# Attention steps of two heads from each key group, with score products that alternate between the two halves of the array's rows

## What is computed

```
proj = h @ w_in + b_in                     # 16 query heads, 2 key/value heads, 64 wide
q = q.reshape(B, NB, 128, Hkv, G, dh) * dh ** -0.5        # Hkv = 2 groups of G = 8 heads
kc, vc = with_prev(k), with_prev(v)        # a block sees itself and the one before: 256 keys
s = einsum('bnqhgd,bnkhd->bnhgqk', q, kc)  # scores, masked to a window of 128
mx = maximum(max(s, -1), sink)             # one learned sink logit per head
p = exp(s - mx)
p = p / (sum(p, -1) + exp(sink - mx))
o = einsum('bnhgqk,bnkhd->bnqhgd', p, vc).reshape(B, S, Hq * dh)
return o @ w_out + b_out
```

## Time and profile before

| | |
|---|---|
| runs | 1165.36, 1166.43, 1445.92 us; median 1166.43 |
| span of the profiled execution | 1163.4 us (its own time is not given) |
| PE busy | 1142.8 us, 98% |
| DVE, ACT busy | 543.2 us (47%), 431.8 us (37%) |
| mean granted TensorE clock | 0.998 of full speed |
| moved by DMA | 105.06 MB, 90 GB/s over the span |

### The profile page before, as it was taken

The page is one execution under the profiler, slowest core; times in us unless marked ns, Lnnn a source line. Parts: engine busy times, 40 slices in busy tenths (PEclk is TensorE's granted clock), DMA queues, the critical chain, the costliest instruction groups (busy, mean ns, idle before and its releaser), DMA issues.

```text
span 1163.4 us, 15354 instructions
## 1 busy us (share of the span) xinstructions
PE 1142.8 (98%) x5833; PEld 966.2 (83%) x5833; DVE 543.2 (47%) x834; ACT 431.8 (37%) x748; POOL 13.3 (1%) x22
## 2 busy tenths in 40 slices
PE   6999999999999999999999999999999999999997
PEld 6888888898888888888889988889888888888886
DVE  5424467854434434433365565555534434433344
ACT  6410325543332332323354365544332332323242
POOL 0000001000000000000000000000000000000000
PEclk9999999999999999999999999999999999999999
DMA  8233212323233233122262522002333233212241
GB/s 238 58 91 91 69 59 73 109 73 95 86 108 97 83 108 102 43 82 99 90 181 57 161 74 73 1 1 73 109 108 103 78 108 104 76 52 93 90 145 72
DMA packets 142855, 105.06 MB, mean 90 GB/s; under 512 B 22054, under 2 KB 130784, under 8 KB 142816
## 3 DMA queue, kind: packets, MB, share of 16 engines
q1 hardware_dynamic: 142816, 104.52, 30.1%
HBM read 102.41 MB, written 2.10 MB: 90 GB/s over the span
## 4 chain that ended last, share of the span: by engine, by line
PE 93%; DVE 3%; ACT 2%; DMA 1%; issue 0%; SPq 0%; DVEq 0%; ACTq 0%
PE ps L1298 18%; PE ps L1300 18%; PE ps L1299 18%; PE ps L1534 6%; PE ps L1535 6%; PE ps L1533 6%; PE ps L1611 2%; PE ps L1638 2%; PE ps L1478 2%; PE ps L1480 2%; PE ps L1479 2%; PE ps L1363 1%; PE ps L1365 1%; PE ps L1364 1%; PE ps L1622 1%; PE ps L1434 1%
## 5 line engine op out<-in xcount | busy, mean ns | idle before, releaser
L1298 PE MATMUL ps<-act_hi,w_hi 128*128 128x512 f32 (+1 forms) x1072 | 387.7, 362 | 1.4 <-DVE act_lo L841 1.4
L1299 PE MATMUL ps<-act_lo,w_hi 128*128 128x512 f32 (+1 forms) x1072 | 385.3, 359 | 0.0
L1300 PE MATMUL ps<-act_hi,w_lo 128*128 128x512 f32 (+1 forms) x1072 | 385.2, 359 | 0.0
L1298 PEld LDWEIGHTS ps<-act_hi,w_hi 128*128 128x128 f32 x1072 | 202.8, 189 | 33.4 <-DVE act_lo L841 2.2
L1299 PEld LDWEIGHTS ps<-act_lo,w_hi 128*128 128x128 f32 x1072 | 202.9, 189 | 29.9
L1300 PEld LDWEIGHTS ps<-act_hi,w_lo 128*128 128x128 f32 x1072 | 202.8, 189 | 30.0
L1533 PE MATMUL ps<-w_hi 128*128 128x512 f32 x288 | 112.0, 389 | 0.0
L1534 PE MATMUL ps<-w_lo,w_hi 128*128 128x512 f32 x288 | 112.0, 389 | 0.0
L1535 PE MATMUL ps<-w_hi,w_lo 128*128 128x512 f32 x288 | 112.0, 389 | 0.0
L664 ACT ACTIVATE arena<-ps,vecs 128x512 f32<-128x512 f32 x44 | 34.3, 779 | 188.9 <-PE ps L1300 188.9
L489 ACT CAST w_hi<-raw 128x1024 fp32r<-128x1024 f32 x71 | 73.4, 1046 | 81.6 <-PE ps L1300 45.0
(11 more groups left out here) (167 smaller groups left out, 1228.0 us busy)
## 6 DMA issues: line engine op xcount, KB each, us to landing
raw<-in_f_w_up SPq DMA_DIRECT2D x88, 512.0 KB, 4.3
raw<-in_f_w_down SPq DMA_DIRECT2D x44, 512.0 KB, 3.3
raw<-in_m_w_in SPq DMA_DIRECT2D x24, 512.0 KB, 3.8
raw<-in_m_w_out SPq DMA_DIRECT2D x8, 512.0 KB, 3.3
raw<-in_a_w_in SPq DMA_DIRECT2D x16, 256.0 KB, 4.4
raw<-in_a_w_out SPq DMA_DIRECT2D x8, 512.0 KB, 4.4
h<-in_x SPq DMA_DIRECT2D x4, 512.0 KB, 5.1
out<-h SPq DMA_DIRECT2D x3, 512.0 KB, 2.6
```

What stands on the lines that cost most here:

```text
L1298: nc.tensor.matmul(dst, lh, rh, start=(i == 0), stop=False)
L1299: nc.tensor.matmul(dst, lh, rl, start=False, stop=False)
L1300: last = nc.tensor.matmul(dst, ll, rh, start=False, stop=(i == n - 1))
```

## The change

A step takes the query tiles 2n and 2n + 1 of its block (n = s % 4), that is heads 2n, 2n + 8, 2n + 1 and 2n + 9 in this order, so its score products go to rows 0 to 63, 64 to 127, 0 to 63, 64 to 127. Key group g writes bank g. The sinks are read with a stride, each head of the mix takes its own group's values, and `o_tok` holds the heads in the order of the steps. So the rows of the output projection's weights are loaded in that order, by two DMAs of 64 rows each for a unit instead of one of 128, and `DMAS` counts two.

```
-    for q in [G_GATE] + [G_AIN + n for n in range(A_UNITS) if A_TILE[n] < KT]:
+    for q in [G_GATE] + [G_AIN + n for n in range(A_UNITS) if A_TILE[n] < KT] \
+            + [G_AOUT + k for k in range(KT)]:
         DMAS[q] = 2
...
-        GROUPS = [0, 2, 1, 3]
+        def pair(s, j):
+
+            return s // ASTEPS, s % ASTEPS * 2 + j // KVH, j % KVH
...
                 load_free(G_AOUT + k)
-                load(G_AOUT + k, a_w_out[0, k * P:(k + 1) * P])
+                s = SLOT[G_AOUT + k] % 4
+                for g in range(KVH):
+                    r0 = (k + KT * g) * DH
+                    nc.sync.dma_start(raw[g * DH:(g + 1) * DH, s], a_w_out[0, r0:r0 + DH])\
+                        .then_inc(raw_in[s], 16)
...
             def sink_cols(s):
-                n = GROUPS[s % ASTEPS]
-                return sink[:, n * AG:(n + 1) * AG]
+                n = s % ASTEPS
+                return sink[:].rearrange("p (g t) -> p t g", g=KVH)[:, 2 * n:2 * n + 2]
+
+            def by_pair(cols):
+                return cols.rearrange("p (t g) -> p t g", g=KVH)
...
                 for j in range(AG):
+                    _, t, g = pair(s, j)
+                    h0 = t + KT * g
                     ins = nc.vector.tensor_tensor_reduce(
-                        out=sc[:, b, j, lo:], in0=ps[:, j // 2, (j % 2) * 2 * P + lo:(j % 2 + 1) * 2 * P],
-                        in1=band[:, lo:], scale=DH ** -0.5, scalar=sink_cols(s)[:, j:j + 1],
+                        out=sc[:, b, j, lo:],
+                        in0=ps[:, g, (t % 2) * 2 * P + lo:(t % 2 + 1) * 2 * P],
+                        in1=band[:, lo:], scale=DH ** -0.5, scalar=sink[:, h0:h0 + 1],
                         op0=ALU.add, op1=ALU.max, accum_out=asm[:, b, 0, j:j + 1])
                 link(ins)
-                nc.vector.tensor_tensor(asm[:, b, 3], sink_cols(s), asm[:, b, 0], ALU.subtract)
+                nc.vector.tensor_tensor(by_pair(asm[:, b, 3]), sink_cols(s), by_pair(asm[:, b, 0]),
+                                        ALU.subtract)
...
             def scores(s):
-                blk, n = s // ASTEPS, GROUPS[s % ASTEPS]
-                g = n * AG // KT
-                pr = slice(g * DH, (g + 1) * DH)
+                blk = s // ASTEPS
...
                 for j in range(AG):
-                    t = (n * AG + j) % KT
-                    dst = ps[:, j // 2, (j % 2) * 2 * P + lo:(j % 2 + 1) * 2 * P]
+                    _, t, g = pair(s, j)
+                    pr = slice(g * DH, (g + 1) * DH)
+                    dst = ps[:, g, (t % 2) * 2 * P + lo:(t % 2 + 1) * 2 * P]
...
             def mix(s):
-                b, blk, n = s % 2, s // ASTEPS, GROUPS[s % ASTEPS]
-                g = n * AG // KT
+                b, blk = s % 2, s // ASTEPS
...
                 for j in range(AG):
+                    g = pair(s, j)[2]
```

More of the change, by code:

```diff
@@ L1228, in normalised @@
             def normalised(s):
-                b, blk, n = s % 2, s // ASTEPS, GROUPS[s % ASTEPS]
+                b, blk, n = s % 2, s // ASTEPS, s % ASTEPS
                 dve.wait_ge(pv_mm, s + 1)
```

## The result

The changed kernel takes 1156.11 us (median of 4 runs, 1154.79 to 1156.15), the kernel before 1166.08 in the same comparison. The ratio is 0.9912, 95% interval 0.9898 to 0.9927: 10.0 us less by the medians, where the prediction had 7.7. The median of the kernel before counts one execution of 1445.92 us; without it, it is 1165.73, and the first set too shows 9.6 us less. The profiled execution took 1156.1 us for a span of 1154.3, 1.8 us above it.

What follows compares the result with a forecast made beforehand. PE, busy 98% of the span, was taken as the bound; 7.74 us less from overlapping score passes, all else 0, took the span from 1163.4 to 1155.7, time 1158.7 us (chance 0.50), range 1156 to 1168.

Steps and rivals of the forecast that it cites:

- part 1: Score products alternating between row halves: passes overlap, a stretch falls from 1.92 to 1.28 us, 7.74 us over 12 steps.
- No overlap: Rival for the score passes: both halves share one stream, 0.215 us a pass stays, time 1166.4; chance 0.18.
- late weights: Rival for the score passes: a half's first weight load starts late, halving the overlap, time 1162.4; chance 0.15.
- an emptying at each change of half: Rival in the score stretch: 0.20 us three times a step, 9.6 us lost, time 1176.0; chance 0.14.
- starts stay in order: Assumption for the score passes: starts keep program order, so eight passes need five slots of 0.215 us, 0.645 less a step.
- Block 0: Its four steps with 128-column score passes: loads as long as streams, so no gain, stretch still about 1.1 us.
- overlapping loads: Rival: weight loads of different halves overlap too, block 0 included, 1.3 us more gain, time 1157.4; chance 0.03.
- part 3: Whether DVE and ACT keep up: ACT's copy before the mix has 0.81 us slack, 0.17 left, so the saving holds.
- part 4: Loads of w_out, 16 of 256 KB for 8 of 512 KB: each unit some 0.4 us later, covered, cost 0.
- part 5: DVE's strided read of sink columns, once a step: even at 0.48 us covered by 0.67 us of slack.
- The offset of 3.0 us: Median time 1166.43 taken as 3.0 above the profiled span of 1163.4, added to the forecast span of 1155.7.
- about 2%: Difference a measurement of this kernel tells from no change (1143 and 1190 us); within it 0.98.

Runs made afterwards that it cites:

- the run with the halves in turn: Changed kernel with a step's score products in head order 0, 2, 1, 3, four passes in rows 0 to 63, then four in 64 to 127: 1155.98 us.
- second set: The changed kernel measured again, unedited, beside the kernel before: 1155.69 us against 1165.31, ratio 0.9917.
- the run with the late mix: Changed kernel with a step's mix put behind the first unit of that step's output products, where there are any: 1158.46 us, ratio 0.9939.

## Why the prediction was right and wrong

- **What bounds the kernel, and that the scores count one to one:** right. PE stays busy 98%, and 10.2 us less between the first and last score pass make a span 9.1 shorter with a start 1.0 later.
- **Overlap of the two halves at all (part 1):** right, and the rivals fall. No overlap and late weights would have left stretches of 1.92 and 1.6 us, an emptying at each change of half over 2.4; it is 1.06. The exposed load and the emptying at the change of shape stayed: 1.06 is 0.105 + 4 x 0.215 + 0.095.
- **The size of the overlap: the step that failed.** The step was "starts stay in order", from which I counted five slots for U U L L U U L L. The passes fill four, because each half works through its own products and does not wait for the other's; the order of the program inside a step is free, as the run with the halves in turn shows. The term was 3 x 0.215 = 0.645 us a step and measured 0.86; over 12 steps 10.3 us, not 7.74. The range went wrong with it: its lower end, 1156, was built on five slots, and 1156.11 just lies in it while the second set's 1155.69 does not. (A reading beside it was loose too: eight starts have seven distances, of 0.126 us on average with the longer first one, not 0.110. The last start, 126.05, is right all the same.)
- **Block 0: wrong.** I put the gain at nothing, since loads and streams are equally long there, and gave overlapping loads 0.03 of chance and 1.3 us as upper end. The loads of the two halves do overlap: 0.45 us in each of four steps, 1.8 in all, more than that upper end, again because four slots remain and not five.
- **The cover on ACT (part 3): the number was right, and the larger saving went past it.** I had 0.81 us of slack before the mix and wrote that past it the copy would be the bound. With 0.86 it is. Between the first and the last score pass that returns 0.11 us in eight steps and 0.1 in two of block 0 (whose 0.39 us of slack I had not counted), 1.1 us; once more it comes behind the last. The other 0.8 lies in steps 6 and 7, where the stage hangs on ACT and DVE (copy, exponentials, act_hi, act_lo, then L1224), as the chain shows:

```profile
687.02 1.01 ACT arena L740
...
690.60 0.69 DVE act_lo L1259
...
693.53 2.08 ACT arena L731 x8
...
696.08 1.01 ACT arena L740
697.09 0.04 issue
697.13 2.00 PE ps L1651 x16
```

  From the one copy to the next this takes 9.1 us. In the kernel before, the same two copies start 9.1 us apart as well:

```profile
689.29 1.01 ACT L733 COPY arena<-ps 128x1024 f32<-128x1024 f32 x1 [2.31 <-PE ps L1622]
...
697.88 0.56 ACT L740 CAST act_hi<-ps 128x512 fp32r<-128x512 f32 x1
698.43 1.01 ACT L733 COPY arena<-ps 128x1024 f32<-128x1024 f32 x1
```

  There too the second copy began as soon as the act_hi cast ahead of it was done. So in this stretch ACT and DVE had no slack even before, and part 3, which looked at one later step and at the sum of ACT's busy time, missed it. In the page's chain over the whole span DVE has 4% and ACT 3% now, in place of 3% and 2%.
- **The loads (part 4) and DVE's strided read (part 5):** cost 0, right (L1230 takes 0.16 us as L1217 did). That the second unit would be 0.4 us later was wrong: it is 1.7 with the two DMAs alone and 2.1 in the changed kernel, because I counted only the issues and took the transfers to be as fast as before.
- **The sum:** 12.1 gross less 1.9 given back is 10.2; I had 7.7 gross and nothing back. Two errors of opposite sign, of which the first was the larger; that they partly cancel is luck. The offset of 3.0 us between span and time was too large as well: in the executions on record it is 1.7 to 1.9, in the kernel before too, so its span of 1163.4 belongs to an execution of some 1165.2 us (an estimate), below the three times given with it.
- **What a measurement can tell:** I said about 2%. The comparison resolved 0.9912 to within 0.15%, so a gain under 1% stands clear of the scatter.

The Trainium skill (TensorE: Matmul & The Clock Gate, "Part 3: Packing small matmuls") has starts about 4 ns apart for tiles in distinct row groups. The starts within 0.01 us here agree with it. The same part says that products start in strict program order. For products in different halves the measurement decides against it: in the run with the halves in turn, a pass starts ahead of three others that stand before it in the program.

## What to carry to other kernels

Products with 64 rows of contraction stream in half the time here if, between two changes of shape, the two halves of the rows have equally many of them (they also wrote different PSUM banks), and that where weight loads set the pace too; the 0.20 us of the changes of shape stay. Two orders among them gave the same time. Before counting the gain, take the smallest slack behind the shortened stretch and compare it with the largest gain, not the likeliest, and look at every step for it, not at one. Where an evacuation then becomes the bound, try releasing it by halves before moving PE's work: here it gained 2.3 us, while the work that was moved had been filling another wait.

## What the runs showed of the hardware that I had not expected

- Two f32 products in different halves of the rows run side by side at full speed, 256 columns in 0.215 us a pass each, and two weight loads of 128 columns run side by side too, both in 0.19 us.
- A product of one half overtakes products of the other half that stand ahead of it in PE's program, by at least three passes (the run with the halves in turn: eight passes within 1.07 us).
- A pause of PE of 2.15 us in a busy stage (688.38 to 690.53 us in the run with the late mix) was followed by a stretch at a granted clock of 0.51, with products at 0.43 us in place of 0.23. The changed kernel, whose longest wait between the score passes is 0.5 us, has 1.00 throughout the stage.
